# Weight splits moved off GpSimd, a SiLU in place of sigmoid and products, and four split buffers in a mixture-of-experts layer

## What is computed

```python
def expert_block(args):            # xb: rows routed to expert e, in blocks
    xb, e = args
    gu = xb @ w_gate_up[e] + b_gate_up[e]          # 1024 -> 2048
    gate, up = jnp.split(gu, 2, axis=-1)
    gate = jnp.minimum(gate, 7.0)
    up = jnp.clip(up, -7.0, 7.0)
    glu = gate * jax.nn.sigmoid(1.702 * gate)
    return ((up + 1.0) * glu) @ w_down[e] + b_down[e]   # 1024 -> 1024
```

## Time and profile before

| | us |
|---|---|
| median of 3 runs | 1673.26 (1668.55 to 1675.0) |
| span of the profiled execution | 1669.1 |
| PE busy | 1480.9 (89%) |
| DVE busy | 1358.4 (81%) |
| ACT busy | 1008.6 (60%) |
| POOL busy | 906.1 (54%) |
| DMA, mean over the span | 457.41 MB, 274 GB/s |

### The profile page before, as it was taken

One profiled execution on the slowest core, in us unless ns is written; L12 is line 12 of the kernel. 1 busy time (PEld: TensorE's weight loads), 2 busy tenths in 40 slices (PEclk: granted clock), 3 DMA queues, 4 the chain that ended last, 5 costly groups with the idle time before them and its releaser, 6 DMA issues.

```text
span 1669.1 us, 22226 instructions
## 1 busy us (share of the span) xinstructions
PE 1480.9 (89%) x6727; PEld 1199.1 (72%) x6727; DVE 1358.4 (81%) x1216; ACT 1008.6 (60%) x934; POOL 906.1 (54%) x562
## 2 busy tenths in 40 slices
PE   6998998699999999999999999999999999999983
PEld 6864687577777777777777777777777777777772
DVE  5566545488999888999888899988899988899982
ACT  5437543376666666666666666666666666666662
POOL 3200351476555776655776655577655577655573
PEclk9999997899999999999999999999999999999996
DMA  9211035478888888888888888888888888888874
GB/s 268 102 49 51 1 120 214 165 282 326 325 322 319 317 321 326 326 324 316 317 326 324 325 323 318 319 318 326 318 321 321 319 323 321 321 321 323 312 263 127
DMA packets 103003, 457.41 MB, mean 274 GB/s; under 512 B 22407, under 2 KB 23486, under 8 KB 70142
## 3 DMA queue, kind: packets, MB, share of 16 engines
q1 hardware_dynamic: 92270, 427.41, 67.0%
q0 software_dynamic: 10704, 29.64, 8.0%
HBM read 442.85 MB, written 23.59 MB: 279 GB/s over the span
## 4 chain that ended last, share of the span: by engine, by line
PE 52%; DVE 21%; issue 16%; ACT 8%; DMA 1%; DVEq 0%; ACTq 0%; POOL 0%; SPq 0%; POOLq 0%
PE ps L724 21%; PE ps L727 10%; DVE wlo L1270 9%; ACT whi L976 7%; PE ps L456 5%; DVE uc L1380 4%; PE ps L762 3%; PE ps L611 3%; PE ps L711 2%; DVE XT_lo L1362 2%; DVE uc L1385 2%; DVE gc L1372 1%; PE ps L510 1%; PE ps L481 1%; PE ps L669 1%
## 5 line engine op out<-in xcount | busy, mean ns | idle before, releaser
L1552 POOL TENSOR_TENSOR wlo<-raw,whi 128x384 fp32r<-128x384 f32 x256 | 476.8, 1870 | 273.2 <-ACT whi L976 270.3
L1270 DVE TENSOR_TENSOR wlo<-raw,whi 128x1664 fp32r<-128x1664 f32 x256 | 529.7, 2090 | 74.0 <-ACT whi L976 73.7
L976 ACT ACTIVATE whi<-raw 128x2048 fp32r<-128x2048 f32 x256 | 486.6, 1913 | 135.5 <-PE ps L727 128.3
L1270 DVE TENSOR_TENSOR wlo<-raw_more,whi 128x1664 fp32r<-128x1664 f32 x128 | 281.6, 2208 | 67.9 <-ACT whi L976 67.8
L1552 POOL TENSOR_TENSOR wlo<-raw_more,whi 128x384 fp32r<-128x384 f32 x128 | 274.8, 2154 | 51.9 <-ACT whi L976 51.6
L976 ACT ACTIVATE whi<-raw_more 128x2048 fp32r<-128x2048 f32 x128 | 245.6, 1919 | 78.9 <-PE ps L727 74.9
L724 PE MATMUL ps<-whi,XT_hi 128*128 128x512 f32 x1024 | 287.0, 403 | 1.0 <-issue 1.0
L724 PE MATMUL ps<-whi,XT_lo 128*128 128x512 f32 x1024 | 274.9, 390 | 0.0
L727 PE MATMUL ps<-wlo,XT_hi 128*128 128x512 f32 x1024 | 274.1, 389 | 0.0
L724 PEld LDWEIGHTS ps<-whi,XT_hi 128*128 128x128 f32 x1024 | 199.0, 197 | 43.7 <-issue 1.4
L724 PEld LDWEIGHTS ps<-whi,XT_lo 128*128 128x128 f32 x1024 | 193.6, 189 | 41.6
(11 more groups left out here) (288 smaller groups left out, 1788.6 us busy)
## 6 DMA issues: line engine op xcount, KB each, us to landing
raw<-in_w_gate_up_dram SPq DMA_DIRECT2D x192, 1024.0 KB, 6.1
raw_more<-in_w_gate_up_dram SPq DMA_DIRECT2D x64, 1024.0 KB, 6.4
raw_more<-in_w_down_dram SPq DMA_DIRECT2D x64, 1024.0 KB, 7.0
raw<-in_w_down_dram SPq DMA_DIRECT2D x64, 1024.0 KB, 6.8
raw<-in_w_in_dram SPq DMA_DIRECT2D x6, 1024.0 KB, 10.5
raw<-in_w_out_dram SPq DMA_DIRECT2D x4, 1024.0 KB, 4.9
xnat<-in_x_dram SPq DMA_DIRECT2D x4, 512.0 KB, 5.3
x<-in_x_dram POOLq DMA_DIRECT2D x4, 512.0 KB, 5.6
```

What stands on the lines that cost most here:

```text
L976: S.activation(whi[:, k % SPL, :], xraw(k), ACT.Copy).then_inc(hi_done, 1)
L1270: Vv.tensor_tensor(wlo[:, k % SPL, 0:DVE_COLS], xraw(k)[:, 0:DVE_COLS], whi[:, k % SPL, 0:DVE_COLS], ALU.subtract).then_inc(lo_dve, 1)
L1552: G.tensor_tensor(wlo[:, k % SPL, DVE_COLS:], xraw(k)[:, DVE_COLS:], whi[:, k % SPL, DVE_COLS:], ALU.subtract).then_inc(lo_pool, 1)
```

## The change

- GpSimd splits nothing any more. VectorE makes the low part of all 2048 columns, in the expert stage and before it. The semaphore `lo_pool` is gone everywhere.
- The split buffers in the expert stage are four (`MSL`), the fourth being `whi_more` and `wlo_more` in memory that was free; chunks are split four ahead (c from 4 to 15 of an iteration) instead of two. Before the stage four expert chunks are split: two as before, two after the copies to `h2T` on ScalarE (VectorE's part: at the start of `one_pass`).
- The activation: ScalarE computes silu(1.702 gate) of 128x1024 straight from PSUM into `glu` (`gated`). Silu(1.702 g) is 1.702 g x sigmoid(1.702 g), so clamping it at `GLU_MAX` is the clamp of the gate, and the factor 1/1.702 goes into the copies to HT_hi and HT_lo. The bias of the up half has 1 added once, by a new GpSimd instruction before the stage, so VectorE clamps up + 1 to -6 and 8 in one instruction and makes min(glu, GLU_MAX) x up in a second (`activated`). Both stand before the split of c = 11, with `rows_high` and `rows_low` behind them; `table` moves behind c = 8.
- GpSimd's queue keeps `gather` and `scatter` alone.

The diff, cut to its core (what is left out are buffer and semaphore declarations and the same replacement in `down`):

```diff
 CHUNK = 2048
 RAW, SPL = 4, 3
 XRAW = 6
-DVE_COLS = 1664
+MSL = 4
...
-def block_of(n):
-
-    return (4 * SMALL, 1408) if n < 2 else (CHUNK, DVE_COLS)
+def width_of(n):
+
+    return 4 * SMALL if n < 2 else CHUNK
...
-        gc = at("gc", RA + 16384, [P, 2, 512])
-        sg = at("sg", RA + 20480, [P, 2, 512])
+        whi_more = at("whi_more", RD, [P, CHUNK], F32R)
+        wlo_more = at("wlo_more", RA + 16384, [P, CHUNK], F32R)
+        glu = at("glu", RE + 12288, [P, 2, 512])
...
+
+        def whi_of(k):
+
+            s = (k - N0) % MSL
+            return whi[:, s, :] if s < SPL else whi_more[:, :]
+
+        def wlo_of(k):
+
+            s = (k - N0) % MSL
+            return wlo[:, s, :] if s < SPL else wlo_more[:, :]
...
                 if free:
                     sp.wait_ge(lo_dve, n0 + (k - free + 1))
-                    sp.wait_ge(lo_pool, n0 + (k - free + 1))
                 sp.dma_start(xraw(k).rearrange("p (k n) -> p k n", k=parts), src).then_inc(xraw_in[k % XRAW], 16)
...
             def gate_up(E, X, D, e, n0, k0):
 
                 pe.wait_ge(selg_ok, X + 1)
-                pe.wait_ge(uc_ok, past(2 * E))
+                pe.wait_ge(glu_ok, past(E))
+                pe.wait_ge(uc_ok, past(E))
                 for m in range(4):
...
-                    s = (k0 + c) % SPL
+                    Wh, Wl = whi_of(k0 + c), wlo_of(k0 + c)
                     high_ready(n0 + (k0 + c))
                     for l in (XT_hi, XT_lo):
                         for m in range(4):
-                            T.matmul(ps[:, m, :], l[:, c, :], whi[:, s, m * 512:(m + 1) * 512], start=False, stop=False)
+                            T.matmul(ps[:, m, :], l[:, c, :], Wh[:, m * 512:(m + 1) * 512], start=False, stop=False)
...
                     for m in range(4):
-                        ins = T.matmul(ps[:, m, :], XT_hi[:, c, :], wlo[:, s, m * 512:(m + 1) * 512],
+                        ins = T.matmul(ps[:, m, :], XT_hi[:, c, :], Wl[:, m * 512:(m + 1) * 512],
                                        start=False, stop=c == GUC - 1)
                     ins.then_inc(split_used, 1)
...
             act.wait_ge(bias_in, 64)
+            act.wait_ge(bias_up, 1)
             S.activation(biasB[0:64, :], biasR[0:64, :], ACT.Copy).then_inc(bias_hi, 1)
+            def split_high(w0, k):
+                act.wait_ge(xraw_in[k % XRAW], w0 + 16 * ((k - N0) // XRAW + 1))
+                S.activation(whi_of(k), xraw(k), ACT.Copy).then_inc(hi_done, 1)
+
             def high_x(n0, w0, k):
 
-                act.wait_ge(split_used, n0 + (k - SPL + 1))
-                act.wait_ge(xraw_in[k % XRAW], w0 + 16 * ((k - N0) // XRAW + 1))
-                S.activation(whi[:, k % SPL, :], xraw(k), ACT.Copy).then_inc(hi_done, 1)
+                act.wait_ge(split_used, n0 + (k - MSL + 1))
+                split_high(w0, k)
 
             def presplit(n0, w0):
-                high_x(n0, w0, N0)
-                high_x(n0, w0, N0 + 1)
-
-            presplit(0, 0)
+                for k in range(N0, N0 + MSL):
+                    high_x(n0, w0, k)
+
+            for k in (N0, N0 + 1):
+                act.wait_ge(split_used, k - SPL + 1)
+                split_high(0, k)
...
+            act.wait_ge(split_used, N0)
+            split_high(0, N0 + 2)
+            split_high(0, N0 + 3)
...
             def hidden_high(E):
                 act.wait_ge(ht_pe, E + 1)
-                S.activation(both(HT_hi), ps[:, 6:8, :], ACT.Copy).then_inc(ht_hi, 1)
+                S.activation(both(HT_hi), ps[:, 6:8, :], ACT.Copy, scale=1.0 / ALPHA).then_inc(ht_hi, 1)
...
-            def sigmoid(E, f):
-                act.wait_ge(gc_ok, 2 * E + f + 1)
-                S.activation(sg[:, f, :], gc[:, f, :], ACT.Sigmoid, scale=ALPHA).then_inc(sg_ok, 1)
+            def gated(E, done):
+
+                act.wait_ge(split_used, done)
+                S.activation(glu[:, :, :], ps[:, 0:2, :], ACT.Silu, scale=ALPHA).then_inc(glu_ok, 1)
...
             def one_pass(r):
                 E0, X0, n0, w0 = r * NE, r * (NE + 1), r * PASS, r * (16 * PASS // XRAW)
                 select(0, sel_gu, selg_ok, gub_pe, E0)
-                high_x(n0, w0, N0 + 2)
                 rows_high(X0)
-                for c in range(GUC):
-                    if c >= 3:
-                        high_x(n0, w0, N0 + c)
-                    if c == 3:
+                for c in range(MSL, EC):
+                    if c == EC - 1:
+                        gated(E0, n0 + (N0 + GUC))
+                        rows_high(X0 + 1)
+                    high_x(n0, w0, N0 + c)
+                    if c == 5:
                         select(1, sel_gu, selg_ok, gub_pe, E0 + 1)
-                rows_high(X0 + 1)
-                sigmoid(E0, 0)
-                sigmoid(E0, 1)
-                high_x(n0, w0, N0 + GUC)
-                high_x(n0, w0, N0 + GUC + 1)
                 hidden_high(E0)
                 with act.Fori(1, NE) as e:
                     E, X = E0 + e, X0 + e
                     ne, we = n0 + e * EC, w0 + e * (16 * EC // XRAW)
-                    for c in range(2, EC + 2):
+                    for c in range(MSL, EC + MSL):
+                        if c == EC - 1:
+                            gated(E, ne + (N0 + 2 * GUC - EC))
+                            rows_high(X + 1)
                         high_x(ne, we, N0 + GUC - EC + c)
-                        if c == 3:
+                        if c == 5:
                             select(e + 1, sel_gu, selg_ok, gub_pe, E + 1)
-                        if c == 5:
+                        if c == 7:
                             select(e - 1, sel_dn, seld_ok, dnb_pe, E - 1)
-                        if c == 10:
-                            rows_high(X + 1)
-                            sigmoid(E, 0)
-                        if c == 11:
-                            sigmoid(E, 1)
                     hidden_high(E)
                     weighted(E - 1, e - 1)
                 select(NE - 1, sel_dn, seld_ok, dnb_pe, E0 + (NE - 1))
-                high_x(n0, w0, N0 + PASS - 2)
-                high_x(n0, w0, N0 + PASS - 1)
                 act.wait_ge(split_used, n0 + (N0 + PASS))
                 weighted(E0 + (NE - 1), NE - 1)
...
             def low_x(n0, k):
                 dve.wait_ge(hi_done, n0 + (k + 1))
-                Vv.tensor_tensor(wlo[:, k % SPL, 0:DVE_COLS], xraw(k)[:, 0:DVE_COLS], whi[:, k % SPL, 0:DVE_COLS],
-                                 ALU.subtract).then_inc(lo_dve, 1)
+                Vv.tensor_tensor(wlo_of(k), xraw(k), whi_of(k), ALU.subtract).then_inc(lo_dve, 1)
...
+                for k in range(N0, N0 + MSL):
+                    low_x(n0, k)
+
+            low_x(0, N0)
+            low_x(0, N0 + 1)
...
             def hidden_low(E):
                 dve.wait_ge(ht_hi, past(E + 1))
-                Vv.tensor_tensor(both(HT_lo), ps[:, 6:8, :], both(HT_hi), ALU.subtract).then_inc(ht_lo, 1)
-
-            def clamp(E, done):
+                Vv.scalar_tensor_tensor(out=both(HT_lo), in0=ps[:, 6:8, :], scalar=1.0 / ALPHA, in1=both(HT_hi),
+                                        op0=ALU.mult, op1=ALU.subtract).then_inc(ht_lo, 1)
...
+            def activated(E, done):
 
                 dve.wait_ge(split_used, done)
-                for f in range(2):
-                    Vv.tensor_scalar(gc[:, f, :], ps[:, f, :], LIMIT, None, ALU.min).then_inc(gc_ok, 1)
-                    Vv.tensor_scalar(uc[:, f, :], ps[:, 2 + f, :], LIMIT, -LIMIT, ALU.min, ALU.max).then_inc(uc_ok, 1)
-
-            def hidden(E):
-
-                dve.wait_ge(uc_ok, past(2 * E + 2))
-                dve.wait_ge(gc_ok, 2 * E + 2)
-                for f in range(2):
-                    Vv.scalar_tensor_tensor(out=uc[:, f, :], in0=uc[:, f, :], scalar=1.0, in1=gc[:, f, :],
-                                            op0=ALU.add, op1=ALU.mult).then_inc(t_ok, 1)
-                dve.wait_ge(t_ok, 2 * E + 2)
-                for f in range(2):
-                    dve.wait_ge(sg_ok, 2 * E + (f + 1))
-                    Vv.tensor_tensor(uc[:, f, :], uc[:, f, :], sg[:, f, :], ALU.mult).then_inc(h_act, 1)
+                Vv.tensor_scalar(uc[:, :, :], ps[:, 2:4, :], LIMIT + 1.0, 1.0 - LIMIT, ALU.min, ALU.max).then_inc(uc_ok, 1)
+                dve.wait_ge(uc_ok, past(E + 1))
+                dve.wait_ge(glu_ok, past(E + 1))
+                Vv.scalar_tensor_tensor(out=uc[:, :, :], in0=glu[:, :, :], scalar=GLU_MAX, in1=uc[:, :, :],
+                                        op0=ALU.min, op1=ALU.mult).then_inc(h_act, 1)
...
-                low_x(n0, N0 + 2)
+                if isinstance(r, int):
+                    low_x(n0, N0 + 2)
+                    low_x(n0, N0 + 3)
                 rows_low(X0)
                 table(D0 + 1, 1, bank=5)
-                for c in range(GUC):
-                    if c >= 3:
-                        low_x(n0, N0 + c)
-                    if c == 2:
+                for c in range(MSL, EC):
```

(51 more changed lines are left out.)

46 lines of the change are left out of this document (17 added, 29 removed).

## The result

The changed kernel takes 1508.6 us (median of 4 runs, 1504.8 to 1515.9) where the one before takes 1672.2; the ratio is 0.9034, with an interval from 0.9003 to 0.9065. The forecast was 1524 us with a range of 1503 to 1578: the direction, the size and the range were right, and the forecast was 15 us too careful. The profiled execution of after has a span of 1505.7 us.

The account below looks back on a forecast made before the run. TensorE bounds the expert periods, with a wait for `uc` and a slow clock behind it. 30 x (41.51 - 36.7) = 144.3, + 3.6 + 2.8 - 1.0 = 149.7 us off 1673.3 gives 1524 us, range 1503 to 1578.

Parts of the forecast that it names:

- (a): Weight splits in the expert stage and before: VectorE takes all 2048 columns, GpSimd none; each split takes 2.29 us.
- (b): Activation: one SiLU 1.2 us, one clamp 1.22, one product 1.28; product done at T+4.2, T being the end of gate-up.
- (c): Four split buffers, splits four chunks ahead, activation between splits of chunks 10 and 11; nothing late, 8 us slack.
- VectorE's sum: VectorE's new work per expert period: 34.1 us, below TensorE's 35.9.
- (d): Weight loads in the expert periods: DMA needs 35.7 to 36.3 us beside TensorE's 35.9, so a period of 36.7.
- (e): First expert's activation, with no down product beside it: 9.1 us becomes 5.5, a gain of 3.6.
- (f): End after the last period: 3.6 us of waiting goes, 0.8 is lost waiting for HT_lo; net gain about 2.8.
- (g): Stretch before the experts, with longer VectorE splits: a cost of 1.0 us, between 0.5 and 5.
- R1: Rival: DMA or HBM binds harder in the periods; period 38.3 us, time 1572 us; chance 13%.
- R2: Rival: VectorE splits stay at 2.72 us although GpSimd is quiet; period 39.2 us, time 1599 us; chance 5%.
- R3: Rival: the product still comes after the down chunks; period about 40.5 us, time 1638 us; chance 4%.
- R4: Rival: TensorE's clock falls without its pauses; slower than before, 1715 us at 1.2 GHz for 0.2 of the time; chance 4%.

Follow-up runs that it names:

- (b) and (c): Changed kernel, but GpSimd again splits 384 columns of each chunk in the expert stage; 1509.9 us, period 36.06 us.
- (a) with (c): Changed kernel, but with the old activation (four clamps, two sigmoids, four products); 1514.1 us, period 36.06 us.
- The eight kernels: All combinations of the change's three parts, the kernel before and the changed kernel among them; compared by period, from 36.06 to 43.25 us.
- (a) and (b): Changed kernel, but with three split buffers and the splits two chunks ahead; 1505.6 us, period 36.06 us.
- (c) alone: Kernel before, with four split buffers, splits four ahead and the old activation moved; GpSimd still splits in the expert stage; 1729.4 us, period 43.25 us.
- the run with 1 MB more: Changed kernel plus 1 MB of weight loads per expert into a tile that nothing reads; 1517.6 us, mean period 36.19 us.

## Why the prediction was right, point by point

- **What bounds the kernel** was right: TensorE with the wait for `uc` and the slow clock behind it. The full-clock price of a period, put at 35.9 us from the rows, measured 36.06.
- **(a) The split's cost** was right: 2.29 forecast, 2.29 measured. All splits of the group lie between 2.28 and 2.30 us, and none at 2.7. The Trainium skill ("SBUF — State Buffer", "Who interferes with whom") says that the exclusive lock needs a GpSimd instruction on the same port pair; this trace agrees with it, since with GpSimd down to its requests VectorE's second mode in the earlier trace rows is gone. The prediction's "little between" was a misreading for GpSimd, though: the median of its row is 1.68 us, and about a third of its splits in the expert stage of before take 1.1 to 1.9. And the runs correct the weight that I gave the lock: with the lock fully in place, parts (b) and (c) reach 36.06 too.
- **(b) The activation** was right in each term: clamp 1.22 (1.22), product 1.23 (1.28), SiLU 1.02 (1.2), done at T+4.2 as the walk said, hidden transposes without a wait. ScalarE's 27.3 us and no table load per period, as forecast.
- **VectorE's sum** was 1.2 us too high, 34.1 against 32.9, nearly all of it because durations of neighbours overlap. Here this cost nothing. In the expectation for (a) with (c) the same error turned the answer.
- **(c) The order** was right for the change as a whole: nothing late. The eight kernels show what the walk alone could not: with (a) and (b) the fourth buffer isn't needed, and part (c) by itself harms.
- **(d) DMA** is the step that failed, though within its range: 36.7 us were taken and 36.06 measured, which makes 19 us over 30 periods. The need of 35.7 us came from 373 GB/s in a stretch with share 1.00, taken for capacity. It was demand: 396 GB/s went through in the same stage. "Two limits that nearly coincide don't reach the larger one exactly" had no second limit. The Trainium skill ("DMA: Bandwidth & Descriptors", "Specifications") states about 358 GB/s per core, from which 1539 us would follow; the row of after has 370 over 1082 us and the run with 1 MB more 396, and the measurement decides.
- **(e) and (f), the first expert and the end**, were right to 0.1 and 0.5 us. The last down product waits for ScalarE's selection, not for HT_lo as I had named: the mechanism had the right size and the wrong name.
- **(g) Before the experts**: 7.2 us instead of 1.0. I counted the longer splits on the chain (0.8 us) but not the clock that falls behind the longer pauses, nor that the freed buffers' loads meet the gather. 4.8 us are the former, up to the first `dispatch` (293.56 to 298.40). 2.4 are the gather: 2.0 by the loads and 0.4 by its request, which ends later beside a longer VectorE split. The term was mis-sized because the clock and the gather stood in it at nothing.
- **The rivals.** R1 (p = 38.3) and R2 (39.2) didn't come, nor R3. R4, the clock, neither: it is 1.00 over all 1082 us of uninterrupted work.
- **The signs.** Idle time before the hidden transposes none from the second expert on, VectorE near 34 (32.9), DMA share 0.98 with 370 GB/s, GpSimd under 12%: as said. The clock of the whole span, 0.97, stayed below the 0.98 that I asked for, by the front.

## What to carry to other kernels

When one engine is bound and the others are 63 to 89% busy, as here, a loss in the loop often has several sufficient cures. Build the combinations before crediting a part: here any two of three reached the floor, and one alone made it 4% slower. Check also that a part is one thing: (c) was a buffer and an order. Don't read a full DMA share as capacity: add a load and see whether anything waits. Small steps ahead of the loop (who splits there, what runs beside a gather that TensorE waits for, where the first activation stands) were worth another 1% when the loop had nothing left. One short stretch there differed by 7 us between traces by the clock, so read the clock of both before crediting an edit.

## What the hardware showed that I had not expected

- A VectorE split of 1.89 us took 5.13 us beside three GpSimd splits in a row (3.47 us of them). One neighbour lengthened it to 2.7 at most (in (b) with (c) a third of the splits lie in between, at 2.0 to 2.3); several in a row held it off for as long as they lasted.
- The DMA moved 396 GB/s over 1084 us at a share of 1.02 (so a share near 1 doesn't say how much room is left), and up to 422 GB/s in a stretch of 2 us.
- The gather of 128 rows took TensorE 4.4 us of waiting with neither a weight load nor a VectorE split near it, 5.7 beside a VectorE split of 1.89 us without a load (request 2.26 instead of 1.12 us), and 8.0 beside a split of 2.29 (request 2.64) with one load of 1 MB started 1.9 us behind it.
- TensorE's clock fell from 1.00 to 0.79 in two stretches of 8 us before the experts, in a chain of short steps in which a VectorE split had grown from 1.80 to 2.20 us. Behind the same pause of 1.85 us it fell in after and not in (c) alone.
